# A first unit of work wholly in fp32, its transfers in five pieces, and the tables sent after the second unit's weights

## The reference

```
a = rmsnorm(h, norm_mix_pre[0]) @ w_dqkv       # 1024 -> 384 + 256 + 32
c_q, c_kv, k_rope = split(a)
c_q, c_kv = rmsnorm(c_q, q_norm), rmsnorm(c_kv, kv_norm)
q = c_q @ w_uq;  kv = c_kv @ w_ukv             # then rope, causal attention, w_o
```

## Time and profile before

| | |
|---|---|
| runs | 898.83, 899.99, 897.97 us; median 898.83 |
| span of the profiled execution | 896.4 us; the median of the runs stands 2.4 us above it |
| PE busy | 882.7 us, 98% |
| DVE, ACT, POOL busy | 675.9, 503.2 and 163.6 us |
| transfers | 146.81 MB, mean 164 GB/s |

### The profile page before, as it was taken

One profiled execution on the slowest core, in us unless ns is written; L12 is line 12 of the kernel. 1 busy time (PEld: TensorE's weight loads), 2 busy tenths in 40 slices (PEclk: granted clock), 3 DMA queues, 4 the chain that ended last, 5 costly groups with the idle time before them and its releaser, 6 DMA issues.

```text
span 896.4 us, 19632 instructions
## 1 busy us (share of the span) xinstructions
PE 882.7 (98%) x7222; PEld 857.7 (96%) x7222; DVE 675.9 (75%) x1167; ACT 503.2 (56%) x853; POOL 163.6 (18%) x158
## 2 busy tenths in 40 slices
PE   9999999999999999999999999999999999999997
PEld 8977889999999998899999999999999999999997
DVE  7768459999994446999999544889888788875556
ACT  6777665666665347766666535554455444444443
POOL 0029530000001004200000003200032333313312
PEclk9999999999999999999999999999999999999999
DMA  7652134545455631354456454344434555564441
GB/s 251 197 126 88 58 132 158 177 181 187 167 213 184 236 152 47 107 189 182 180 187 223 168 204 158 118 166 141 141 142 171 196 188 185 186 229 176 170 141 48
DMA packets 25778, 146.81 MB, mean 164 GB/s; under 512 B 3040, under 2 KB 9216, under 8 KB 10496
## 3 DMA queue, kind: packets, MB, share of 16 engines
q1 hardware_dynamic: 25584, 145.99, 46.0%
q10 hardware_dynamic: 144, 0.13, 0.0%
HBM read 142.84 MB, written 1.05 MB: 161 GB/s over the span
## 4 chain that ended last, share of the span: by engine, by line
PE 94%; DVE 3%; ACT 1%; DMA 1%; issue 1%; POOL 0%; SPq 0%; DVEq 0%; POOLq 0%
PE bank L519 27%; PE bank L520 26%; PE bank L521 26%; PE bank L868 2%; PE bank L1091 1%; PE bank L884 1%; PE bank L657 1%; PE bank L672 1%; PE bank L902 1%; PE bank L640 1%; PE bank L812 1%; DMA k_heads<-w_dq_dram 1%; PE bank L1048 1%; PE bank L557 1%; PE bank L551 1%
## 5 line engine op out<-in xcount | busy, mean ns | idle before, releaser
L519 PE MATMUL bank<-u_high,w_high 128*128 128x256 f32 (+2 forms) x1318 | 376.6, 286 | 2.7 <-ACT u_high L1254 1.2
L520 PE MATMUL bank<-u_low,w_high 128*128 128x256 f32 (+2 forms) x1318 | 374.1, 284 | 0.0
L521 PE MATMUL bank<-u_high,w_low 128*128 128x256 f32 (+2 forms) x1318 | 373.0, 283 | 0.0
L519 PEld LDWEIGHTS bank<-u_high,w_high 128*128 128x128 f32 x1318 | 248.9, 189 | 5.7 <-ACT m L1226 1.7
L520 PEld LDWEIGHTS bank<-u_low,w_high 128*128 128x128 f32 x1318 | 248.6, 189 | 0.0
L521 PEld LDWEIGHTS bank<-u_high,w_low 128*128 128x128 f32 x1318 | 248.4, 188 | 0.0
L1675 DVE TENSOR_TENSOR w_low<-raw,w_high 128x1024 fp32r<-128x1024 f32 (+6 forms) x106 | 181.2, 1710 | 88.9 <-ACT w_high L1208 87.4
L1208 ACT ACTIVATE w_high<-raw 128x1024 fp32r<-128x1024 f32 (+6 forms) x115 | 179.9, 1565 | 66.8 <-PE bank L521 62.5
L519 PE MATMUL bank<-x_high,w_high 128*128 128x256 f32 (+1 forms) x592 | 167.9, 284 | 0.4 <-DVE x_low L2257 0.3
L521 PE MATMUL bank<-x_high,w_low 128*128 128x256 f32 (+1 forms) x592 | 168.2, 284 | 0.0
L520 PE MATMUL bank<-x_low,w_high 128*128 128x256 f32 (+1 forms) x592 | 167.3, 283 | 0.0
(11 more groups left out here) (290 smaller groups left out, 1140.4 us busy)
## 6 DMA issues: line engine op xcount, KB each, us to landing
raw<-w_up_dram SPq DMA_DIRECT2D x66, 1024.0 KB, 4.8
raw<-w_down_dram SPq DMA_DIRECT2D x24, 1408.0 KB, 5.9
raw<-w_gin_c_dram SPq DMA_DIRECT2D x4, 1536.0 KB, 6.7
raw<-w_wo_dram SPq DMA_DIRECT2D x4, 1024.0 KB, 5.4
raw<-w_wout_dram SPq DMA_DIRECT2D x4, 1024.0 KB, 4.7
raw<-w_pgate_dram SPq DMA_DIRECT2D x4, 1024.0 KB, 4.8
raw<-w_gin_v_dram SPq DMA_DIRECT2D x2, 1024.0 KB, 4.7
raw<-w_gin_g_dram SPq DMA_DIRECT2D x2, 1024.0 KB, 5.5
```

What stands on the lines that cost most here:

```text
L519: nc.tensor.matmul(out, hi, rhi, start=start, stop=False)
L520: nc.tensor.matmul(out, hi, rlo, start=False, stop=False)
L521: return nc.tensor.matmul(out, lo, rhi, start=False, stop=stop)
```

## The change

The pieces become five, of 1, 1, 2, 2 and 2 chunks. Unit 0 has no split part any more: all 24 tiles are fp32 products. `BY_SCALAR` names the chunks whose product with the gain ACT makes; the last two of these products give the signals that the split of unit 0 gave. The sums of a0 stand before chunk 7, the rows of a0 before chunk 1 of unit 1. On SP, ident and the tables are issued after a wait for the landing of unit 1. On ACT, the high part of unit 2 stands before the wait for the tables.

```diff
+BY_SCALAR = (1, 2, 4, 6)
-PIECES = DC // 2
+PIECES = ((0,), (1,), (2, 3), (4, 5), (6, 7))
...
-            w = UNITS[0]["tiles"] * P // PIECES
-            return [slice(p * w, (p + 1) * w) for p in range(PIECES)]
+            w = UNITS[0]["tiles"] * P // DC
+            return [(slice(cs[0], cs[-1] + 1), slice(cs[0] * w, (cs[-1] + 1) * w)) for cs in PIECES]
...
             sp.dma_start(par[:, 0:DC], dram["par"][:, 0:DC]).then_inc(gains_in, 16)
-            for p, cols in enumerate(first_pieces()):
-                sp.dma_start(h[:, 2 * p:2 * p + 2, :], dram["h0"][:, 2 * p:2 * p + 2, :]).then_inc(h_in[p], 16)
+            for p, (chunks, cols) in enumerate(first_pieces()):
+                sp.dma_start(h[:, chunks, :], dram["h0"][:, chunks, :]).then_inc(h_in[p], 16)
                 sp.dma_start(first_weights[:, cols], dram["w_dq"][0, :, cols])\
-                    .then_inc(loaded[0] if p == PIECES - 1 else pieces_in[p], 16)
-            sp.dma_start(ident[:, :], dram["ident"]).then_inc(ident_in, 16)
+                    .then_inc(loaded[0] if p == len(PIECES) - 1 else pieces_in[p], 16)
...
                         if n == 1:
+                            sp.wait_ge(loaded[1], 16)
+                            sp.dma_start(ident[:, :], dram["ident"]).then_inc(ident_in, 16)
                             for dst, src_ in ((par[:, DC:NPAR], dram["par"][:, DC:NPAR]),
                                               (rope[:, :, :], dram["rope"]), (cmask[:, :], dram["cmask"])):
                                 sp.dma_start(dst, src_).then_inc(tables_in, 16)
...
             for k in range(DC):
                 if k == DC - 2:
+                    pe.wait_ge(loaded[0], 16)
                     parts_ready(n)
-                    norm_sums("a0", f"a0 acc {DC - 1}", squares(0, T1))
-                if k >= DC - 2:
-                    u_ready("a0")(k)
-                else:
-                    if k % 2 == 0:
-                        pe.wait_ge(pieces_in[k // 2], 16)
+                for p, chunks in enumerate(PIECES[:-1]):
+                    if k == chunks[0]:
+                        pe.wait_ge(pieces_in[p], 16)
+                if k < DC - 2:
                     pe.wait_ge(*done(f"a0 u {k}"))
                 if k == DC - 1:
-                    pe.wait_ge(ident_in, 16)
-                    norm_rows("a0", token_rows(R_BANK, T1))
+                    norm_sums("a0", f"a0 acc {DC - 1}", squares(0, T1))
                 for b in range(3):
                     out = bank[BLOCKS[b]["bank"]][:, 0:T1]
-                    if k >= DC - 2:
-                        last = three(out, *weights(n, 3 * k + b), uh[:, k, :], ul[:, k, :], False, k == DC - 1)
-                    else:
-                        tile = slice((3 * k + b) * P, (3 * k + b + 1) * P)
-                        nc.tensor.matmul(out, first_weights[:, tile], first_u[:, k, :], start=k == 0, stop=False)
+                    tile = slice((3 * k + b) * P, (3 * k + b + 1) * P)
+                    last = nc.tensor.matmul(out, first_weights[:, tile], first_u[:, k, :], start=k == 0, stop=k == DC - 1)
...
+            def first_rows():
+                pe.wait_ge(ident_in, 16)
+                norm_rows("a0", token_rows(R_BANK, T1))
             unit(n + 1, T1, (uh, ul), u_ready("a0"), first_low="second unit low",
-                 between={6: lambda: latent_sums("cq", 0, OVER_Q), 7: lambda: norm_rows("cq", latent_rows(R_BANK))})
+                 between={1: first_rows, 6: lambda: latent_sums("cq", 0, OVER_Q), 7: lambda: norm_rows("cq", latent_rows(R_BANK))})
...
-            for p in range(PIECES):
-                c = 2 * p
+            for p, chunks in enumerate(PIECES):
                 act.wait_ge(h_in[p], 16)
-                if p < PIECES - 1:
-                    nc.scalar.activation(first_u[:, c, :], h[:, c, :], ACT.Copy, scale=pcol("mix_pre0", c))\
-                        .then_inc(*S.step(f"a0 u {c}"))
...
+                for c in chunks:
+                    if c in BY_SCALAR:
+                        nc.scalar.activation(first_u[:, c, :], h[:, c, :], ACT.Copy, scale=pcol("mix_pre0", c))\
+                            .then_inc(*(S.step(f"a0 u {c}") if c < DC - 2 else (high_parts, 1)))
...
-            cols = first_pieces()[PIECES - 1]
-            act.wait_ge(loaded[0], 16)
-            nc.scalar.activation(wh[0][:, cols], first_weights[:, cols], ACT.Copy).then_inc(high_parts, 1)
             high(1, first="second unit", middle=lambda: rms("a0", 3))
+
+            n = FIRST_UNIT["dq"]
+            high(n + 2)
             act.wait_ge(tables_in, 48)
             act.wait_ge(ident_in, 16)
-
-            n = FIRST_UNIT["dq"]
-            high(n + 2)
...
-            cols = first_pieces()[PIECES - 1]
-            dve.wait_ge(high_parts, 1)
-            nc.vector.tensor_tensor(wl[0][:, cols], first_weights[:, cols], wh[0][:, cols].bitcast(F32), ALU.subtract)\
-                .then_inc(low_parts_v, 1)
             norm("a0", tiles_of(T1))
             low(1, None, "second unit", lambda: keep_rows("a0", T1))
```

More of the change, by code:

```diff
@@ L253, in program @@
         tables_in, ident_in = sem("tables_in"), sem("ident_in")
-        h_in = [sem(f"h_in_{c}") for c in range(PIECES)]
-        pieces_in = [sem(f"first_unit_in_{c}") for c in range(PIECES - 1)]
+        h_in = [sem(f"h_in_{c}") for c in range(len(PIECES))]
+        pieces_in = [sem(f"first_unit_in_{c}") for c in range(len(PIECES) - 1)]
         gains_in = sem("first_gains_in")
@@ L1371, in _ @@
             act.wait_ge(gains_in, 16)
-            for p in range(PIECES):
-                c = 2 * p
+            for p, chunks in enumerate(PIECES):
                 act.wait_ge(h_in[p], 16)
-                if p < PIECES - 1:
-                    nc.scalar.activation(first_u[:, c, :], h[:, c, :], ACT.Copy, scale=pcol("mix_pre0", c))\
-                        .then_inc(*S.step(f"a0 u {c}"))
-                for k in (c, c + 1):
+                for c in chunks:
+                    if c in BY_SCALAR:
+                        nc.scalar.activation(first_u[:, c, :], h[:, c, :], ACT.Copy, scale=pcol("mix_pre0", c))\
+                            .then_inc(*(S.step(f"a0 u {c}") if c < DC - 2 else (high_parts, 1)))
+                for k in chunks:
                     square("a0", k, h[:, k, :], T1, S.step(f"a0 sq {k}"))
-                for k in (c, c + 1):
+                for k in chunks:
                     nc.scalar.activation(uh[:, k, :], h[:, k, :], ACT.Copy, scale=pcol("mix_pre0", k))\
                         .then_inc(*S.step(f"a0 u high {k}"))
-            cols = first_pieces()[PIECES - 1]
-            act.wait_ge(loaded[0], 16)
-            nc.scalar.activation(wh[0][:, cols], first_weights[:, cols], ACT.Copy).then_inc(high_parts, 1)
             high(1, first="second unit", middle=lambda: rms("a0", 3))
+            n = FIRST_UNIT["dq"]
+            high(n + 2)
             act.wait_ge(tables_in, 48)
             act.wait_ge(ident_in, 16)
-            n = FIRST_UNIT["dq"]
-            high(n + 2)
             def latent_squares(js):
@@ L1880, in _ @@
             dve.wait_ge(gains_in, 16)
-            for p in range(PIECES):
-                c = 2 * p + 1
+            for p, chunks in enumerate(PIECES):
                 dve.wait_ge(h_in[p], 16)
[L1884 to L1887, removed]
+                for c in chunks:
+                    if c not in BY_SCALAR:
+                        nc.vector.tensor_scalar(first_u[:, c, :], h[:, c, :], pcol("mix_pre0", c), None, ALU.mult)\
+                            .then_inc(*(S.step(f"a0 u {c}") if c < DC - 2 else (low_parts_v, 1)))
+                for k in chunks:
                     dve.wait_ge(*done(f"a0 sq {k}"))
@@ L1891, in _ @@
                         .then_inc(*S.step(f"a0 acc {k}"))
-                for k in (c - 1, c):
+                for k in chunks:
                     u_low("a0", k, T1, 0, "mix_pre0")
-            cols = first_pieces()[PIECES - 1]
-            dve.wait_ge(high_parts, 1)
-            nc.vector.tensor_tensor(wl[0][:, cols], first_weights[:, cols], wh[0][:, cols].bitcast(F32), ALU.subtract)\
-                .then_inc(low_parts_v, 1)
             norm("a0", tiles_of(T1))
```

## The result

The changed kernel takes 902.27 us (median of 5 runs, 900.27 to 902.9), the kernel before 898.83 (5 runs, 897.83 to 899.99): 3.4 us more, a ratio of 1.004 with the 95% interval 1.0028 to 1.0051. The profiled execution took 902.9 us, the slowest of the five, and spans 901.1.

The account below looks back on a forecast made before the run. TensorE, busy 98%, was taken as the bound, with PE and DVE meeting at 22.7. DVE's late low half of unit 2 stalls the PE, shifting everything +2.25: 898.83 becomes 901.1, clock staying full; range 900.2 to 903.0.

Parts of the forecast that it names:

- A: The forecast case: PE stall of 1.9 before the cq sums, clock stays full, shift +2.25, 901.1; chance 0.47.
- B: Rival: same stall, but the clock falls in it, adding +1.2 (0.7 to 2.1): 902.3; chance 0.30.
- the stall of 1.9: PE idle before the first latent norm's sums (L820): ready at 23.1, going on at 24.95.
- the end of the trace: After its last matmul the PE stopped at 890.4; granted clock full until 891.9, then 0.5; cited for a fall.
- Price of the fall: Cost of a lowered clock in the PE's products around and behind the stall: +1.2 (0.7 to 2.1).
- Shift of the sums: Start of the first latent norm's sums (L820) on the PE: 24.95 instead of 22.71, +2.25.
- SP's four issues: SP issues ident, par, rope and the mask in 2.52 before w_dkr, whose issue moves from 14.65 to 16.8.
- The wait of 0.6 ahead of chunk 2: PE in unit 0: chunks 0 and 1 end at 7.8, next piece taken at 8.4, so the early start is lost.
- C: Rival: piece 2 and w_dkv land early (7.8 and 12.4), unit 1 0.6 sooner, +1.65: 900.5; chance 0.15.
- Landing of w_dkv: Transfer queue without ident and tables ahead or sharing: 0.2 sooner, landing 14.2, range 12.4 to 14.5.
- Fp32 unit: PE, chunks 6 and 7 of unit 0: 0.62 more work in fp32 passes; the 0.49 idle before the sums goes.
- Five pieces: Front of unit 0: PE starts 0.35 sooner, lost in a wait; later w_dkv issue (5.70 to 5.95) hidden.

Follow-up runs that it names:

- run 4: The changed kernel measured again on one chip with runs 5, 6 and 7: 902.33, +4.1 to the kernel before (ratio 1.0052).
- run 1: The changed kernel with ident and the tables issued early again, without SP's wait for w_dkv: 901.16, +3.0 to the kernel before (ratio 1.0036).
- run 2: The kernel before with only ident and the tables moved behind the landing of w_dkv: 901.15, +3.0 (ratio 1.0032).
- run 9: The kernel before with only the rows of a0 moved from unit 0 to ahead of chunk 1 of unit 1: 900.85, +2.5 (ratio 1.0032).
- run 3: The changed kernel with 16 spare fp32r products filling the PE's stall before the sums of cq: 900.68, +2.5 to the kernel before (ratio 1.003).
- run 5: The changed kernel, tables still late, with latent squares made and added ahead of unit 2's parts: 899.84, +1.7 to the kernel before (ratio 1.0021).
- run 6: The changed kernel with latent squares first and ident and tables early; rows stay in unit 1: 899.74, +1.55 to the kernel before (ratio 1.0019).
- run 7: The changed kernel with tables early and rows of a0 back in unit 0; fp32 unit 0 and five pieces stay: 898.79, +0.6 to the kernel before.
- run 10: The kernel before with only the five pieces, the last one still split: 898.91, +0.56 (ratio 1.0011).
- run 8: As run 7 but with four pieces of two chunks, leaving only unit 0 wholly in fp32: 897.80, -0.4 to the kernel before (ratio 1.0001).
- run 11: Unit 0 wholly in fp32 alone, measured again: 898.10, -0.25 to the kernel before (ratio 0.9997).

## Why the prediction was right, and where not

The direction, the place and the mechanism of the shift were right. 902.27 lies in the range, but 1.2 above the forecast: I forecast +2.25 and +3.4 came (+4.1 in run 4), because the case that I had held the less likely came in most executions. Point by point:

- *Which case.* The forecast took the clock to stay full (A, 901.1) and gave its fall a chance of 0.30 (B, 902.3). The measured median is B's. The weighing that failed is "the stall of 1.9 is bounded by busy stretches on both sides, which the end of the trace was not". Stalls of 1.5 us with the one-column sums behind them were followed by a fall in the profiles of runs 1, 2, 4 and 9, and the change's 2.25 by one that lasted twice as long. By the mean clock 22 of the 28 executions of these kernels have a fall (4 of 5 of the change, and in runs 1, 2, 4 and 9 3 of 5, 5 of 7, 5 of 5 and 5 of 6); the other six are the fastest ones of their kernels, and the change's own is 900.27. Why it stays out in some is open. The Trainium skill's rule of thumb ("TensorE: Matmul & The Clock Gate", section "Why this matters for your kernels") would leave the clock up after a gap this short. The stalls of 1.5 to 2.25 us in these five profiles don't agree with it; the end of the trace before was the better guide. Run 3, with the stall filled, is A: +2.5 where A has +2.25.
- *Price of the fall.* I took 1.2 (0.7 to 2.1). Between sums and uqn, four profiles lose 1.35 (runs 1, 2, 4, 9: 3.18 - 1.83, 3.31 - 1.95, 3.79 - 2.43, 2.93 - 1.58), and the changed kernel's own loses 2.75, beyond my upper end: the clock was low for 6.8 us in it and for 3.4 in the others. By the mean clocks, 0.998 in the fastest and 0.995 in the slowest, this can account for the spread of its runs, 900.27 to 902.9. The warm-up, by which I sized the fall, stands in the profile with a granted clock of 1.00, so it didn't show the price by itself; the change's rows do: the six ident products of cq's rows take 1.29 at 0.50, and 0.74 in run 3 at 1.00.
- *Shift of the sums.* +2.25 forecast, +2.09 and +2.43 in two profiles. The two lines that meet at unit 2's low half did meet: w_dkr was the later one by 0.64 in one execution, the rows in the other. Within it terms were off and cancelled, by luck. SP's four issues took 1.89, not 2.52: issued late and alone they last 0.33 to 0.43 each, against 0.47 to 0.65 in the earlier trace rows. And w_dkr landed 4.8 after its issue, not 4.2. The wait of 0.6 ahead of chunk 2, which A has and C lacks, was not there in the first profile (rows at 17.97, not 18.7) and was 0.68 in run 4 (rows at 19.05): C's first condition came true in one of the two, and w_dkr held the sums back all the same.
- *Landing of w_dkv.* I took 0.2 gained, to 14.2; it was with ACT at 14.44 and 14.80 against 14.47. Two effects hide in this. With five pieces it is with ACT at 14.44 to 14.80 in the four profiles with late tables (the change, runs 3, 4 and 5) and at 14.71 to 15.70 in the four with early ones (runs 1, 6, 7 and 10). So the tables' absence was worth some 0.7 on the mean, and the five pieces took it back.
- *Fp32 unit.* 0.62 of extra passes against 0.49 of idle removed make +0.13; alone it is at -0.25 and -0.4 (runs 8, 11), and both intervals take in no change. The term was small, as forecast; its sign is open. (The step of a product, 0.126, is right, but 3.77/30 is not how it comes out: the 30 starts from 25.01 to 28.75 are 29 steps in 3.74, of which the first takes 0.21 and the others 0.126.)
- *Five pieces.* Costed at nothing, with the early start lost. Alone they cost 0.56: two more issues push ident and w_dkv, which I called hidden in the queue of transfers, to a later landing, and ACT's order makes the rows wait for it. Calling this hidden was wrong. Beside it stands the piece of chunks 2 and 3: in run 10 the PE goes on with it 1.27 later than before (9.68 against 8.41), where I had it as before.
- *Sum of the parts.* Tables +3.0, rows +2.5, pieces +0.56, fp32 -0.3 make 5.8 where the whole has 3.4 to 4.1. Tables and rows delay the same instruction, and only the later one counts; undoing the tables alone (run 1) gives back 1.1 at most. The rows alone were not undone in the changed kernel.

## What to carry to other kernels

Where two engines arrive at a meeting point together, follow both lines back to all that feeds them: here one transfer and one small PE step each held the whole front, and either of them alone in the kernel before cost +2.5 to +3.0 where the whole change costs +3.4 to +4.1. A wait put on the engine that issues the transfers is a wait for every later transfer in its program. Look at the granted clock behind a new PE stall as well as at the stall's length; where it can't be removed, try spare products in it, as in run 3.

## What was not expected of the hardware

A PE stall of 1.5 us, followed by 0.9 us of one-column products, was followed by a granted clock of 1.2 GHz in four profiles (runs 1, 2, 4, 9), while the wait of 0.97 at 362 us left it full. The fall came 0.9 to 1.6 us after the stall had ended, in the products behind it (in run 9 sums at 24.29, fall at about 25.9), and only after the 2.25 us stall of the change did it come before the PE went on. The same program shows it in some executions and not in others: by their mean clocks, 5 of 7 in run 2.

A DMA issue on SP's queue is not of one length. That of ident lasted 0.33 us when it was issued late, behind the landing of w_dkv. Behind the same eleven earlier issues it lasted 0.43, 0.70 and 1.30 in runs 1, 6 and 7; what makes the difference was not tried.
